# A two-layer trunk on one core: the feature norms, 32 matmuls without a reader, and where the first expert's exponential and combine weights stand

## What is computed

```python
def layer_norm(x, g, b):
    mu = jnp.mean(xf, axis=-1, keepdims=True)
    var = jnp.mean(jnp.square(xf - mu), axis=-1, keepdims=True)
    y = (xf - mu) * lax.rsqrt(var + LN_EPS) * g + b

def swiglu(x, w_gate, w_up, w_down):
    return (jax.nn.silu(x @ w_gate) * (x @ w_up)) @ w_down

def moe_swiglu(x, w_router, w_gate, w_up, w_down):
    probs = softmax(t @ w_router)
    top_p, top_i = lax.top_k(probs, 2)
    combine = one_hot(top_i) weighted with top_p / sum(top_p), summed
    for e in range(8):
        out = out + combine[:, e:e + 1] * swiglu(t, w_gate[e], w_up[e], w_down[e])

for l in range(2):
    h = layer_norm(ALPHA * h + token_mixer(h, ...), ln1_g[l], ln1_b[l])
    h = layer_norm(ALPHA * h + (swiglu or moe_swiglu)(h, ...), ln2_g[l], ln2_b[l])
```

## Time and profile before

| | us |
|---|---|
| median of 3 runs (1920.14 to 1920.96) | 1920.21 |
| the profiled execution, its own time | 1921.43 |
| span of its trace | 1919.7 |
| TensorE busy | 1855.8 |
| VectorE busy | 1383.6 |
| ScalarE busy | 1130.8 |
| mean of the DMA rate | 254 GB/s |

### The profile page before, as it was taken

One profiled execution on the slowest core, in us unless ns is written; L12 is line 12 of the kernel. 1 busy time (PEld: TensorE's weight loads), 2 busy tenths in 40 slices (PEclk: granted clock), 3 DMA queues, 4 the chain that ended last, 5 costly groups with the idle time before them and its releaser, 6 DMA issues.

```text
span 1919.7 us, 28478 instructions
## 1 busy us (share of the span) xinstructions
PE 1855.8 (97%) x11042; PEld 1634.4 (85%) x11042; DVE 1383.6 (72%) x1148; ACT 1130.8 (59%) x883; POOL 7.3 (0%) x17
## 2 busy tenths in 40 slices
PE   8999999899989999998999999999999999999996
PEld 8999999899979899996778888888888888888884
DVE  4655566544554565666788888888888888888886
ACT  4634354533446443455777767776677777777773
POOL 0000000000000000000000000000000000000000
PEclk9999999999999999998999999999999999999998
DMA  8425324444534355254889989999989999899992
GB/s 322 175 90 190 142 104 182 148 160 153 198 120 157 132 185 186 91 188 147 308 347 347 360 341 347 360 357 361 349 339 354 354 369 353 334 356 362 347 362 99
DMA packets 69940, 488.35 MB, mean 254 GB/s; under 512 B 7824, under 2 KB 8336, under 8 KB 11984
## 3 DMA queue, kind: packets, MB, share of 16 engines
q1 hardware_dynamic: 67680, 481.33, 66.9%
q10 hardware_dynamic: 1600, 3.31, 0.6%
q0 software_dynamic: 560, 2.29, 0.4%
HBM read 483.66 MB, written 1.05 MB: 252 GB/s over the span
## 4 chain that ended last, share of the span: by engine, by line
PE 51%; DVE 2%; ACT 1%; issue 0%; DVEq 0%; ACTq 0%
PE ps L638 10%; PE ps L640 10%; PE ps L639 10%; PE ps L944 5%; PE ps L947 5%; PE ps L946 5%; PE ps L930 1%; DVE w_lo L1655 1%; PE ps L965 1%; ACT w_hi L1089 1%; PE ps L882 0%; PE ps L986 0%; ACT L1341 0%; PE ps L987 0%; PE ps L891 0%
## 5 line engine op out<-in xcount | busy, mean ns | idle before, releaser
L1655 DVE TENSOR_TENSOR w_lo<-raw,w_hi 128x2048 fp32r<-128x2048 f32 x336 | 762.8, 2289 | 145.5 <-ACT w_hi L1089 143.8
L1089 ACT ACTIVATE w_hi<-raw 128x2048 fp32r<-128x2048 f32 x336 | 638.9, 1918 | 188.5 <-PE ps L947 96.7
L638 PE MATMUL ps<-hT_hi,w_lo 128*128 128x272 f32 (+1 forms) x1392 | 405.1, 291 | 24.3 <-DVE hT_lo L1608 13.6
L406 DVE TENSOR_TENSOR w_lo<-raw,w_hi 128x2048 fp32r<-128x2048 f32 (+2 forms) x132 | 282.0, 2144 | 189.6 <-ACT w_hi L399 184.5
L639 PE MATMUL ps<-hT_lo,w_hi 128*128 128x272 f32 (+1 forms) x1392 | 403.8, 290 | 0.0
L640 PE MATMUL ps<-hT_hi,w_hi 128*128 128x272 f32 (+1 forms) x1392 | 403.0, 290 | 0.0
L638 PE MATMUL ps<-w_hi,xg_lo 128*128 128x512 f32 x896 | 360.4, 402 | 4.8 <-DVE w_lo L1655 3.1
L640 PE MATMUL ps<-w_hi,xg_hi 128*128 128x512 f32 x896 | 354.6, 396 | 0.0
L639 PE MATMUL ps<-w_lo,xg_hi 128*128 128x512 f32 x896 | 354.5, 396 | 0.0
L399 ACT ACTIVATE w_hi<-raw 128x2048 fp32r<-128x2048 f32 (+2 forms) x132 | 234.1, 1781 | 171.5 <-PE ps L640 137.3
L638 PEld LDWEIGHTS ps<-hT_hi,w_lo 128*128 128x128 f32 x1392 | 266.9, 192 | 28.1 <-issue 17.1
(11 more groups left out here) (266 smaller groups left out, 1828.1 us busy)
## 6 DMA issues: line engine op xcount, KB each, us to landing
raw<-in_dense_units SPq DMA_DIRECT2D x116, 1024.0 KB, 4.9
raw<-in_moe_w_gate SPq DMA_DIRECT2D x112, 1024.0 KB, 6.7
raw<-in_moe_w_up SPq DMA_DIRECT2D x112, 1024.0 KB, 6.9
raw<-in_moe_w_down SPq DMA_DIRECT2D x112, 1024.0 KB, 6.5
raw<-in_dense_units SPq DMA_DIRECT2D x8, 512.0 KB, 3.9
raw<-in_dense_units SPq DMA_DIRECT2D x8, 256.0 KB, 5.9
srT<-o_tok ACTq DMA_DIRECT2D x6, 272.0 KB, 3.7
hF<-in_x_columns ACTq DMA_DIRECT2D x4, 272.0 KB, 6.3
```

The costliest lines, as they stand in the source:

```text
L406: nc.vector.tensor_tensor(w_lo[:, u % HALVES, 0:k * n], raw[:, u % RAW, 0:k * n], w_hi[:, u % HALVES, 0:k * n].bitcast(F32), ALU.subtract) ...
L638: nc.tensor.matmul(dst, l_lo, r_hi, start=start, stop=False)
L1089: return nc.scalar.activation(dst, src, ACT.Copy, **kw)
L1655: tt(w_lo[:, at % HALVES, :], raw[:, at % RAW, :], w_hi[:, at % HALVES, :].bitcast(F32), ALU.subtract).then_inc(lo_ready, 1)
```

## The change

There are four parts, and a rename (`idle_sqrt` to `idle_col`).

1. **The exponential moves.** `odds` stands now between ScalarE's copies of expert 0's gathered rows and the fourth unit's high half; behind it an activation of one column with SiLU. `combine_and_plan` stands on VectorE behind the third unit's low half. On both engines the gathered rows of expert 1 are copied later: on ScalarE behind the first two units of chunk 1, on VectorE behind `gated` of chunk 0. Six increments of semaphores move from ahead of `places` to ahead of the router's result.
2. **A low half in two parts.** In norms 0 and 1 the low half of the unit for k = 4 to 7, made whole ahead of the centrings until now, is made as two halves of 1024 columns: one at the old place, one behind `low(3)`. TensorE waits for the first with `first_lo_ready`, and for the second when it comes to k = 6. In norm 2 the whole unit moves behind `scale(4)`.
3. **Variance first.** The variance and the reciprocal stand ahead of `centre(0)` and `centre(1)`, which run while ScalarE takes the root; `centre(2)` stands behind `scale(1)`.
4. **32 products.** Behind the sums of each feature norm TensorE issues 32 matmuls on an old high half (`m_hi` or `aT_hi`) into a bank's columns that nobody reads.

```diff
+SPINS = 32
+        def lo_half(dve, u, q):
+            if q == 0:
+                dve.wait_ge(hi_ready, u + 1)
+                dve.wait_ge(units_used, u - HALVES + 1)
+            these = slice(q * UNIT // 2, (q + 1) * UNIT // 2)
+            nc.vector.tensor_tensor(w_lo[:, u % HALVES, these], raw[:, u % RAW, these], w_hi[:, u % HALVES, these].bitcast(F32),
+                                    ALU.subtract).then_inc(lo_ready if q else first_lo_ready, 1)
@@ feature_major (TensorE)
-                    u_hi, u_lo, kn, n = next_unit()
+                    halved = normed if k0 else None
+                    u_hi, u_lo, kn, n = next_unit(halved)
...
+                            if halved is not None and k == kn // 2:
+                                pe.wait_ge(lo_ready, used)
@@ norm_sums (TensorE)
+                still = (m_hi[0], aT_hi)[norm % 2]
+                for _ in range(SPINS):
+                    nc.tensor.matmul(pt[:, 2, cols], still[:, 0, META:META + P], still[:, 0, cols], start=True, stop=True)
@@ odds (ScalarE)
                 nc.scalar.activation(tiny[:, :, 1:2], tiny[:, :, 0:1], ACT.Exp).then_inc(odds_ready, 1)
+                nc.scalar.activation(idle_col[:, :], idle_col[:, :], ACT.Silu)
@@ chunk, expert (ScalarE)
                     hi_of(g, 5, turns, uj + 1)
-                    if gathers:
+                    if gathers or moved:
                         gathered(m, 1)
...
                     gathered(m, 0)
+                    if m == 0:
+                        odds()
                     for i in range(HALVES if m == 0 else 0, 4):
                         hi_of(g, i, 0, u0 + i)
-                    gathered(m, 1)
                     silu(k0, u0 + 2)
-                chunk(1, scatters=seam)
-                if not seam and m == 0:
-                    odds()
+                chunk(1, scatters=seam, moved=not seam)
@@ feature_norm (VectorE)
-                ahead(1)
+                if l == 0:
+                    lo_half(dve, unit_after + 1, 0)
...
                 dve.wait_ge(mean_ready, norm + 1)
-                centre(0)
-                centre(1)
                 full(dve, r)
...
-                centre(2)
+                centre(0)
+                centre(1)
                 dve.wait_ge(deviation_ready, norm + 1)
                 scale(0)
                 scale(1)
+                centre(2)
                 low(0)
...
                 low(3)
+                if l == 0:
+                    lo_half(dve, unit_after + 1, 1)
+                    split.next = unit_after + 2
+                else:
+                    lo(1, NS + 1)
                 low(4)
@@ ahead of the router's result (VectorE), taken from ahead of places(0, 0, (0, 1), 0)
+            for first in (places_ready, gather_lo_ready, hidden_ready, hidden_lo_ready):
+                dve.sem_inc(first, START)
+            dve.sem_inc(result_lo_ready, START + 1)
+            dve.sem_inc(scatter_added, START + 2)
@@ expert (VectorE)
                     for i in range(0 if m else HALVES - 1, 4):
                         lo(i, u0 + i)
-                    gathered(m, 1)
+                        if m == 0 and i == HALVES - 1:
+                            combine_and_plan()
                     for i in range(4, 6):
                         lo(i, u0 + i)
                     gated(k0, u0 + 4)
+                    gathered(m, 1)
                     chunk(1, start=2)
-                    if m == 0:
-                        combine_and_plan()
```

More of the change, by code:

```diff
@@ L210, in ln_col @@
             return par_col(name, norm // 2 * KT + k)
-        idle_sqrt = sb(ctx, "idle_sqrt", [P, 1])
+        idle_col = sb(ctx, "idle_col", [P, 1])
         stats = sb(ctx, "stats", [P, 3, 4, 6])
@@ L345, in trunk @@
         bank_full = sem("bank_full")
+        first_lo_ready = sem("first_lo_ready")
         summed, squared = sem("summed"), sem("squared")
@@ L658, in rowtile, with next_unit @@
                 return x[k // 4][:, k % 4, :] if type(x) is tuple else x[:, k, :]
-            def next_unit():
+            def next_unit(halved=None):
                 nonlocal used
-                pe.wait_ge(lo_ready, used + 1)
+                if halved is None:
+                    pe.wait_ge(lo_ready, used + 1)
+                else:
+                    pe.wait_ge(first_lo_ready, halved + 1)
                 k, n = shape_of(used)
@@ L1128, in squares @@
                 signed_off(r)
-                nc.scalar.activation(idle_sqrt[:, :], idle_sqrt[:, :], ACT.Sqrt)
+                nc.scalar.activation(idle_col[:, :], idle_col[:, :], ACT.Sqrt)
                 ahead()
@@ L1341, in silu, with chunk @@
                     nc.scalar.activation(g_sl[:, :], ps[0][:, 0, :], ACT.Silu).then_inc(silu_ready, 1)
-                def chunk(j, gathers=False, scatters=False, last=False):
+                def chunk(j, gathers=False, scatters=False, last=False, moved=False):
                     uj, k, turns = u0 + (j * UPJ - 2), k0 + j, j - 1
@@ L1525, in deviations, with feature_norm @@
                     settle()
-            def feature_norm(l, names, name, norm, ahead):
+            def feature_norm(l, names, name, norm, unit_after):
                 cols = width(l)
@@ L1544, in feature_norm @@
                 pt = bank(r)
-                ahead(0)
+                if l == 0:
+                    split.upto(unit_after + 1)
+                else:
+                    lo(0, NS)
                 def more(row, a, done=False):
@@ L1658, in _ @@
             step(nc.vector.memset(rstd[:, :, :], 1.0))
-            step(nc.vector.memset(idle_sqrt[:, :], 1.0))
+            step(nc.vector.memset(idle_col[:, :], 1.0))
             settle()
@@ L1853, in _ @@
                             tt(m_lo[c][:, :, width(l)], sgA[s], m_hi[c][:, :, width(l)].bitcast(F32), ALU.subtract).then_inc(dve_done, 1)
-                def next_weights(name, i):
-                    if l == 0:
-                        split.upto(ends[number[l, name]] + i + 1)
-                    else:
-                        lo(i, NS + i)
-                feature_norm(l, ("wo0", "wo1"), "wo_ln", 2 * l, lambda i: next_weights("wo1", i))
+                feature_norm(l, ("wo0", "wo1"), "wo_ln", 2 * l, ends[number[l, "wo1"]])
                 if l == 0:
@@ L1875, in _ @@
                            ALU.subtract).then_inc(dve_done, 1)
-                    feature_norm(l, ("fd0", "fd1"), "fd_ln", 1, lambda i: next_weights("fd1", i))
+                    feature_norm(l, ("fd0", "fd1"), "fd_ln", 1, ends[number[l, "fd1"]])
+            for first in (places_ready, gather_lo_ready, hidden_ready, hidden_lo_ready):
+                dve.sem_inc(first, START)
+            dve.sem_inc(result_lo_ready, START + 1)
+            dve.sem_inc(scatter_added, START + 2)
             r, pt = take(1, "route")
@@ L2060, in add @@
                 tt(h, h, src, ALU.add).then_inc(scatter_added, 1)
-            for first in (places_ready, gather_lo_ready, hidden_ready, hidden_lo_ready):
-                dve.sem_inc(first, START)
-            dve.sem_inc(result_lo_ready, START + 1)
-            dve.sem_inc(scatter_added, START + 2)
             places(0, 0, (0, 1), 0)
```

## The result

| | before | after |
|---|---|---|
| median of the runs beside each other, us | 1920.59 (1920.14 to 1921.38, 4 runs) | 1901.38 (1898.89 to 1907.03, 4 runs) |
| the profiled execution, its own time | 1921.43 | 1900.32 |
| span of its trace | 1919.7 | 1898.6 |
| mean granted clock of TensorE | 0.983 | 0.991 |

The ratio is 0.9904, with a 95% interval of 0.9881 to 0.9927: 1.0% faster, and 0.2 us from the forecast of 1901.2.

A forecast was written before the change was run, and what follows sets the result against it. TensorE, busy 97% of the span, was taken to bound the kernel. Gains of 3.0 (norm 0), 3.1 (norm 1), 2.2 (norm 2, router) and 10.7 (expert 0) sum to 19.0 us: 1901.2 us from 1920.2, range 1898.5 to 1906.

The forecast's parts named there:

- The chain of the norms: Norms 0 and 1: with the variance started earlier, the first product on normed rows comes 1.4 us sooner.
- The wait at k = 2: Norm 0: at full clock TensorE newly waits 0.5 us for the low half of k = 2-3.
- The 32 matmuls: Behind norm sums: 0.125 us each, free under the chain; idle 1.4 us, clock kept, worth 1.6 us in norm 0.
- Rival A: Norms 0 and 1: the clock falls all the same, each loses 1.6 us, giving 1904.4 us; chance 0.12.
- Norm 2 and the router: Last sum of norm 2 to expert 0: 2.2 us gained, bounds 0.7 to 3.5; logits' copy 1.4 to 2.1 us earlier.
- SyncE's later load: The load of the unit six on is issued some 11 us later, covered by five units of about 6 us.
- Expert 0: Start of expert 0: 10.7 us gained from combine work's wait (4.3), table loads (5.6) and first SiLU (0.9); bounds 8.5 to 11.
- the table loads: Expert 0's loop of chunks 2 to 5: two loads per turn go, 4 x 1.39 = 5.6 us gained.
- Rival C: ScalarE stays shut as long again after a table load; TensorE waits about 0.7 us, giving 1901.9 us; chance 0.03.
- B: Rival: expert 0 gets a new wait with half clock in chunk 0, costing 4.3 us, giving 1905.5 us; chance 0.10.
- D: Rival: the 32 matmuls outlast the norms' chain; at 0.62 us each, 24 us slower, 1944 us; chance 0.03.
- E: Rival: the changed program doesn't shed expert 0's loop table loads, giving 1906.8 us; chance 0.02.

The follow-up runs named there:

- E4: The kernel after with the moves at expert 0's start undone, leaving the norms' edits, 32 matmuls and six increments: 1911.38 us, ratio 0.9951 to the kernel before.
- E1: The kernel after without its 32 matmuls behind the sums of each norm: 1903.36 us, ratio 0.9910 to the kernel before.
- E6: The kernel before with the 32 matmuls alone added, the norms' chain as before: 1917.37 us, ratio 0.9982 to the kernel before.
- E9: The kernel after, unchanged, run again as the second set of runs: 1900.05 us against 1918.73 for the kernel before, ratio 0.9898.
- E5: The kernel before with one idle SiLU added behind the exponential at its old place: 1912.65 us, ratio 0.9966 to the kernel before.
- E2: The kernel after with 64 instead of 32 matmuls behind each norm's sums: 1904.74 us, ratio 0.9921 to the kernel before.
- E8: The kernel after with 15 matmuls of 256 columns without a reader between the router's products: 1900.63 us, ratio 0.9904 to the kernel before.
- E10: The kernel after with 40 matmuls per norm, 15 between router products, seven ahead of expert 0's first product, seven in the last down products: 1898.83 us, ratio 0.9892.

## Why the prediction was right

**The chain of the norms: right.** 1.40 us shorter in each (6.80 to 5.40), in every kernel that has it, with the matmuls (E4) and without (E1). The wait at k = 2 was put at 0.5 and is 0.21 us, and not because the row came early: `hT_lo` for k = 2-3 starts 8.09 us behind the last sum (341.36 less 333.27), just as reckoned (346.47 less 1.4 less 336.98). The 24 products of k = 0 and 1 took 3.26 us (338.67 to 341.93) in place of 3.0, so less of the time was left to wait for.

**The 32 matmuls: right in their cost, and right in a clock kept.** 0.135 us apiece in the row (4.32 over 32) where 0.125 was taken. They cover all but 1.44 us of the chain, forecast 1.4, and delay nothing. From first product to first copy the trace has 1.46 and 1.57 us less than the kernel before's, where the prediction had 1.6 for norm 0. Its own terms, 1.9 less 0.5, give 1.4 and not 1.6, so there the sum as written was 0.2 us too high. Against E1 the clock was worth 2.1 and 1.0 us: what it gives depends on when the fall would have begun. Rival A did not come in any of the profiled executions with the whole change. To go by the idle times of 0.77 and 1.72 us came out right, but they promised less than they seemed to: in the kernel after itself the clock fell once behind 1.76 us (at 1871.5), and at 2.8 us it is open (E6). The matmuls alone gave 0.18%; the shortened chain without them (E1) gave 2.8 of the 5.8 us of norms 0 and 1, and the kept clock the rest.

**Norm 2 and the router: the mechanism right, the size off.** The first product comes 1.43 us earlier, the logits' copy 1.41, which is the lower bound given; with the clock down behind the eighth product, VectorE's low half was no limit. `S` comes 0.58 us sooner behind the copy (0.4 reckoned). The logits' copy thus lies 11.26 us behind the last sum and not some 10.6. The step that missed is "the moment at which the clock rises is not mine to set: plus or minus 0.9 us": in the profiled execution after, the clock came back late over the gather, and `S` to expert 0's first product took 8.78 us in place of 7.76, a loss of 1.0. That leaves 1.0 us in place of 2.2. The same kernel in E9 needed 8.11 there and gained 2.0 in all, E1 gained 1.4 and E4 0.8. So a fair figure was 0.8 to 2.0 us, all below the 2.2 taken.

**SyncE's later load** held nothing up: from 330 to 360 and from 547 to 566 us TensorE waits for `hT_lo` alone.

**Expert 0: right.** 10.76 us where 10.7 was taken, 5.60 of it the table loads (E5) and 5.16 the combine work's wait, its half clock and the first SiLU. What the sum could not tell is that 1.5 us of the wait's part are there only when the clock falls behind the old wait: in E4 and E6 it did not. The cover held: on VectorE the combine work ends at 885.11 and the fourth high half, which the next low half needs, at 885.3. Expert 0 had ten table loads in the trace before (898.16 to 988.57) and has two now, none of them in a loop's turn. A turn held up to two, 2.6 us together, of which 1.4 reached TensorE; the rest lay under its products.

**Rival C** (ScalarE shut after a load) did not come. The exponential starts at 880.48, and its load, 1.28 us from 879.19, ended at 880.47. The Trainium skill ("ScalarE: Activation LUTs", "What ACT_TABLE_LOAD costs") adds a drain of about 1380 ns to a switch; no load of expert 0 in either trace shows it, and the measured rows decide. **Rivals B, D and E** did not come; D needed 0.17 us a matmul in norm 0, and E2 shows that even then the loss is at most the time by which they are late (1.8 us for 2.35, and nothing for 3.29 in norm 2).

**The rest** was luck of a kind that the sum could not hold. The forecast stretches gave 17.6 us, the profiled executions differ by 21.1 and the medians by 19.2, 18.7 in the second set. The difference lies in falls of the clock elsewhere, which one execution has and the next not. The kernel before alone ran from 1916.0 to 1926.4 us over the three chips. The kernel after's first four runs follow the granted clock: 1898.89 at 0.992, 1900.32 at 0.991, 1902.45 at 0.990, 1907.03 at 0.986. That a forecast came within 0.2 us of a median with such a spread is luck in its last microseconds: of the 19.0 us, 17.6 were found where they were forecast, 1.2 too many were put on norm 2, and falls elsewhere made up for it.

## What to carry to other kernels

Look at which function ScalarE has loaded when a loop is entered: one idle activation ahead of it took a table load out of every turn of its path and gave 5.6 us. Where TensorE must wait for a short chain, shorten the chain first and then cover most of it with matmuls that nobody reads, and end them before the chain does: they cost nothing until they are late, and then up to their whole lateness. Work of a small helper engine belongs where that engine is idle in the trace, and here the rows priced both parts of that, the table loads and the combine work, to 0.1 us.

## What the runs showed of the hardware

- A fall of the clock can cost nothing: the one at 587.1 to 590.5 in the kernel before only filled 1.5 us in which TensorE would else have waited for ScalarE.
- The clock's fall is not a fixed function of the idle time before it. Behind 2.3 to 2.4 us of idle time it fell in two profiles (before, E5) and not in two (E4, E6); behind 2.75 us it stayed and behind 2.84 it fell, in one execution (E6). Behind the wait of 1.76 to 1.77 us in the last down products it fell in one of ten profiles (the kernel after) and not in E9, the same kernel. And it falls with no such wait at all: at 112.7 to 119.5 in the kernel before TensorE was busy throughout at 0.50, and had no idle time over 0.1 us in the 8 us ahead of it.
- In the kernel after the clock fell 2.8 us into the router (at 862.7), among products of 8 columns and an idle time of 1.03 us (0.57 over 862 to 878). With 15 products of 256 columns between them it stayed at 1.00 until the router's end (E8, E10).
- The Trainium skill ("TensorE: Matmul & The Clock Gate", "What's actually happening") says of the matmuls ahead of the clock's first rise that one kernel shows different numbers of slow ones from run to run. Here the falls in the middle of a kernel differ as well: the kernel after has one at 1873.1 to 1876.5 and none at 763, and in E9, the same kernel, it is the other way (0.50 from 763.5 to 766.9).
